# A stick-breaking attention stage: suffix sums from two f32r parts, one diagonal mask, weight low parts on GpSimd

## The reference

```python
z = jnp.einsum('bhqd,bhkd->bhqk', qb, kb)
before = s_idx < t_idx
log_keep = jnp.where(before, jax.nn.log_sigmoid(-z), 0.0)
log_stick = lax.cumsum(log_keep, axis=3, reverse=True) - log_keep
log_w = jax.nn.log_sigmoid(z) + log_stick
w = jnp.where(before, jnp.exp(log_w), 0.0)
outs.append(jnp.einsum('bhqk,bhkd->bhqd', w, vb))
```

## Time and profile before

| | us |
|---|---|
| median of 3 runs (1935.58 to 1937.6) | 1936.41 |
| the profiled execution | 1935.0 |
| its span, first to last instruction | 1933.3 |
| stick-breaking stage in it, first L1332 to the last matmul before gating | 1542.5 to 1662.3 |

### The profile page before, as it was taken

How to read it: one execution, slowest core, us unless ns; L and a number is a source line. 1 busy time by engine, 2 the same in 40 slices (tenths; PEclk the granted TensorE clock), 3 DMA queues, 4 the chain that set the end, 5 groups by cost and what they waited for, 6 DMA issues and landing times.

```text
span 1933.3 us, 25136 instructions
## 1 busy us (share of the span) xinstructions
PE 1873.5 (97%) x8758; PEld 1490.3 (77%) x8758; DVE 1200.1 (62%) x1844; ACT 799.5 (41%) x1258; POOL 34.1 (2%) x60
## 2 busy tenths in 40 slices
PE   9999999879999999999999999999999999899997
PEld 6888888757888888877777778888887777677875
DVE  7777777745677663356565567767533588665444
ACT  6444444424444442244444444444322355543222
POOL 1000000000000000000000000000000000000000
PEclk9999999999999999999999999999999999999998
DMA  5411211102222232132222132222321311122221
GB/s 202 137 55 56 62 56 33 63 26 88 97 97 87 98 116 90 45 120 76 65 65 75 34 120 97 87 98 76 135 90 60 101 33 66 60 98 87 98 85 57
DMA packets 43407, 158.96 MB, mean 82 GB/s; under 512 B 5489, under 2 KB 5764, under 8 KB 43360
## 3 DMA queue, kind: packets, MB, share of 16 engines
q1 hardware_dynamic: 38592, 143.80, 21.8%
q0 software_dynamic: 4336, 14.47, 2.7%
q10 hardware_dynamic: 432, 0.07, 0.0%
HBM read 155.89 MB, written 6.63 MB: 84 GB/s over the span
## 4 chain that ended last, share of the span: by engine, by line
PE 92%; DVE 4%; ACT 2%; issue 1%; DMA 0%; SPq 0%; DVEq 0%; ACTq 0%
PE acc L504 22%; PE acc L505 22%; PE acc L506 22%; PE acc L528 8%; PE pb L643 2%; PE pc L658 2%; PE pa L808 2%; PE pd L829 1%; PE pa L878 1%; PE pd L890 1%; PE pd L647 1%; ACT wsplit L1010 1%; PE pa L605 1%; PE pa L624 1%; DVE wsplit L1460 1%
## 5 line engine op out<-in xcount | busy, mean ns | idle before, releaser
L504 PE MATMUL acc<-xhi,wsplit 128*128 128x512 f32 x1200 | 505.5, 421 | 8.7 <-DVE wsplit L1460 7.7
L505 PE MATMUL acc<-xlo,wsplit 128*128 128x512 f32 x1200 | 476.3, 397 | 0.0
L506 PE MATMUL acc<-xhi,wsplit 128*128 128x512 f32 x1200 | 476.0, 397 | 0.0
L1010 ACT ACTIVATE wsplit<-wraw 128x1024 fp32r<-128x1024 f32 (+1 forms) x252 | 275.1, 1096 | 455.6 <-PE acc L506 428.8
L1460 DVE TENSOR_TENSOR wsplit<-wraw,wsplit 128x1024 fp32r<-128x1024 f32 (+1 forms) x252 | 320.1, 1274 | 160.8 <-ACT wsplit L1010 158.3
L504 PEld LDWEIGHTS acc<-xhi,wsplit 128*128 128x128 f32 x1200 | 226.6, 189 | 71.9 <-issue 14.0
L505 PEld LDWEIGHTS acc<-xlo,wsplit 128*128 128x128 f32 x1200 | 226.9, 189 | 60.3 <-issue 6.2
L506 PEld LDWEIGHTS acc<-xhi,wsplit 128*128 128x128 f32 x1200 | 226.4, 189 | 55.0
L528 PE MATMUL acc<-xhi,wsplit 128*128 128x512 f32 x464 | 158.3, 409 | 0.0
L506 PE MATMUL acc<-hid_hi,wsplit 128*128 128x512 f32 x352 | 139.5, 396 | 0.0
L505 PE MATMUL acc<-hid_lo,wsplit 128*128 128x512 f32 x352 | 139.5, 396 | 0.0
(11 more groups left out here) (330 smaller groups left out, 2741.4 us busy)
## 6 DMA issues: line engine op xcount, KB each, us to landing
wraw<-w SPq DMA_DIRECT2D x220, 512.0 KB, 3.3
wraw<-w SPq DMA_DIRECT2D x32, 704.0 KB, 4.0
bias_dram<-ext_dram POOLq DMA_DIRECT2D x1, 4096.0 KB, 20.2
bias<-bias_dram POOLq DMA_DIRECT2D x8, 512.0 KB, 4.0
crow<-row_dram POOLq DMA_DIRECT2D x8, 256.0 KB, 3.9
brow<-row_dram POOLq DMA_DIRECT2D x8, 256.0 KB, 4.4
outT<-h SPq DMA_DIRECT2D x8, 256.0 KB, 2.2
h<-xT SPq DMA_DIRECT2D x3, 512.0 KB, 8.7
```

The source lines that it names most:

```text
L504: mm(out, whi[:, k, :], a[:, x_at + k, :], start=(k == first), stop=False)
L505: mm(out, whi[:, k, :], b[:, x_at + k, :], start=False, stop=False)
L506: m = mm(out, wlo[:, k, :], a[:, x_at + k, :], start=False, stop=(k == last))
L1010: A(split(s, j, 0), raw(s, j), ACT.Copy).then_inc(w_hi_ready, 1)
```

## The change

- The softplus goes to a dense double buffer `sp` of 2 x 512 columns by unit parity. ScalarE copies it to `sp_hi` (f32r), VectorE writes `sp_lo` = `sp` - `sp_hi`, and the suffix sum is two f32r matmuls, over `sp_hi` and over `sp_lo`, with an f32r copy `suf` of the triangular matrix.
- The diagonal mask with -1e30 is added to `zs` before |z| is taken, in place of after the suffix sum. The softplus of a masked logit is then zero, so the multiplication with `O_BEFORE` goes, and the exponential of unit t - 3 waits for the subtraction itself.
- The low parts of the weight tiles of stick-breaking blocks 1 to 3 and of the gating stage's first group are made by GpSimd in place of VectorE: twelve tiles. VectorE waits for the last of them before the gating stage.
- The gating stage's four table transfers count on one semaphore; who needs one of them waits for all.

```diff
--- before.py
+++ after.py
@@ -41,7 +41,7 @@
 
 C_ID, C_ONE, C_CUM, C_SUF, C_M1, C_INCL2, C_NEGD, C_LEV = 0, 1, 2, 3, 4, 5, 7, 8
 NCONST = C_LEV + len(LEVELS)
-O_ROWS, O_BEFORE, O_NEGD, O_SUF = range(4)
+O_SUF, O_NEGD = 0, 1
 LAST = 96
 
 
@@ -254,7 +254,8 @@
         yb_hi = r.sb("yb_hi", [P, GPP, S], F32R)
         yb_lo = r.sb("yb_lo", [P, GPP, S], F32R)
         second = r.at
-        order = sb("order", [P, 4, P], at=second - S * 4)
+        order = sb("order", [P, 2, P], at=second - S * 4)
+        suf = sb("suf", [P, P], F32R, at=second - P * 4)
         mg_hi = r.sb("mg_hi", [P, KD, S], F32R)
         mg_lo = r.sb("mg_lo", [P, KD, S], F32R)
         ga = r.sb("ga", [P, 2, S])
@@ -266,7 +267,9 @@
         sk_vt = r.sb("sk_vt", [P, 2, 2, NC, P])
         sk_z = r.sb("sk_z", [P, SBP, S])
         zs = r.sb("zs", [P, 2, TRI])
-        sp = r.sb("sp", [P, 2, TRI])
+        sp = r.sb("sp", [P, 2, S])
+        sp_hi = r.sb("sp_hi", [P, 2, S], F32R)
+        sp_lo = r.sb("sp_lo", [P, 2, S], F32R)
         sw = r.sb("sw", [P, 2, TRI])
         sk_o = r.sb("sk_o", [P, S])
         r = Region(second)
@@ -457,7 +460,7 @@
                 pool.wait_ge(acc_free, st["stick_z"].first)
                 moved = ((slice(0, LAST), slice(0, LAST)), (slice(LAST, LAST + 1), slice(P - 1, P)), (slice(LAST + 1, P), slice(LAST, P - 1)))
                 for to, of in moved:
-                    pool.dma_start(order[to, 0:3, :], consts[of, C_SUF:C_NEGD + 1:2, :]).then_inc(ev("tables_landed"), 16)
+                    pool.dma_start(order[to, :, :], consts[of, C_SUF:C_NEGD + 1:C_NEGD - C_SUF, :]).then_inc(ev("tables_landed"), 16)
                 for e in range(2):
                     other = slice(64 - 64 * e, P - 64 * e)
                     pool.wait_ge(ev("heads_zeroed"), 2 * e + 4)
@@ -466,16 +469,23 @@
                     nc.gpsimd.memset(sk_vt[:, e, :, :, other].rearrange("p b t d -> p (b t) d"), 0.0).then_inc(ev("heads_zeroed"), 1)
                 pool.wait_ge(ev("tables_landed"), 64)
                 for to, of in moved:
-                    nc.gpsimd.tensor_copy(order[:, O_SUF, to], order[:, O_ROWS, of]).then_inc(ev("heads_zeroed"), 1)
+                    nc.gpsimd.tensor_copy(suf[:, to], order[:, O_SUF, of]).then_inc(ev("heads_zeroed"), 1)
+                for i in range(1, SBP + 1):
+                    s, n = (st["stick"], i) if i < SBP else (st["sgu"], 0)
+                    for j in range(3):
+                        pool.wait_ge(w_lo_ready, s.number(n, j))
+                        pool.wait_ge(w_hi_ready, s.number(n, j) + 1)
+                        nc.gpsimd.tensor_tensor(split(s, j, 1), raw(s, j), split(s, j, 0).bitcast(F32), ALU.subtract
+                                                ).then_inc(w_lo_ready, 1)
             if "sgu" in stages:
                 pool.wait_ge(ev("ya_lo_ready"), SBP)
                 pool.wait_ge(acc_free, st["sgu"].first)
-                pool.dma_start(wsp[:], w_spat).then_inc(ev("wsp_landed"), 16)
+                pool.dma_start(wsp[:], w_spat).then_inc(ev("sgu_landed"), 16)
                 for e in range(2):
                     src = b_spat.rearrange("(i e) t -> e i t", e=2)[e]
-                    pool.dma_start(bsp[64 * e:64 * e + 64], src.partition_broadcast(64)).then_inc(ev("bsp_landed"), 16)
-                pool.dma_start(lngb[:], ln_gb.partition_broadcast(P)).then_inc(ev("lngb_landed"), 16)
-                pool.wait_ge(ev("wsp_landed"), 16)
+                    pool.dma_start(bsp[64 * e:64 * e + 64], src.partition_broadcast(64)).then_inc(ev("sgu_landed"), 16)
+                pool.dma_start(lngb[:], ln_gb.partition_broadcast(P)).then_inc(ev("sgu_landed"), 16)
+                pool.wait_ge(ev("sgu_landed"), 64)
 
                 nc.gpsimd.memset(wsp[64:P, :, 0:64], 0.0).then_inc(ev("wsp_ready"), 1)
                 pool.wait_ge(ev("wsp_ready"), 1)
@@ -897,11 +907,12 @@
                     if 2 <= step < units + 2:
                         u = step - 2
                         e, k = u % 2, 3 - u % 8 // 2
-                        pe.wait_ge(ev("sp_ready"), u + 1)
+                        pe.wait_ge(ev("sp_lo_ready"), u + 1)
                         if u >= 2:
                             pe.wait_ge(ev("drest"), u - 1)
-                        mm([pb, pc][u % 2][:, 0:(4 - k) * P], order[:, O_SUF, :], sp[:, e, SEG[k]:SEG[k] + (4 - k) * P],
-                           start=True, stop=True).then_inc(ev("suffix_done"), 1)
+                        out, w = [pb, pc][u % 2], (4 - k) * P
+                        mm(out[:, 0:w], suf[:], sp_hi[:, u % 2, 0:w], start=True, stop=False)
+                        mm(out[:, 0:w], suf[:], sp_lo[:, u % 2, 0:w], start=False, stop=True).then_inc(ev("suffix_done"), 1)
                     if step % 8 == 6 and step < units - 8:
                         turn_v(step // 8 + 1)
 
@@ -1340,8 +1351,12 @@
                     if 3 <= step < units + 3:
                         u, e, k = step - 3, (step - 3) % 2, 3 - (step - 3) % 8 // 2
                         g = slice(SEG[k], SEG[k] + (4 - k) * P)
-                        act.wait_ge(ev("dmasked"), u + 1)
+                        act.wait_ge(ev("drest"), u + 1)
                         A(sw[:, e, g], zs[:, e, g], ACT.Exp).then_inc(ev("sw_ready"), 1)
+                    if 1 <= step < units + 1:
+                        u, w = step - 1, (4 - (3 - (step - 1) % 8 // 2)) * P
+                        act.wait_ge(ev("sp_ready"), u + 1)
+                        A(sp_hi[:, u % 2, 0:w], sp[:, u % 2, 0:w], ACT.Copy).then_inc(ev("sp_hi_ready"), 1)
                     if i < SBP - 1 and v in (2, 5, 7):
                         if v == 7:
                             turned_v(i + 1)
@@ -1844,7 +1859,6 @@
                     if j == 2:
                         dve.wait_ge(ev("heads_zeroed"), 11)
                     take(0, j)
-                    low_ahead(s, 0, j, False)
                 units = 8 * SBP
 
                 for step in range(units + 5):
@@ -1856,6 +1870,9 @@
                         u, e, k = step, step % 2, 3 - step % 8 // 2
                         g = slice(SEG[k], SEG[k] + (4 - k) * P)
                         dve.wait_ge(ev("zs_ready"), u + 1)
+                        tt_(zs[:, e, SEG[k]:SEG[k] + P], zs[:, e, SEG[k]:SEG[k] + P], order[:, O_NEGD, :], ALU.add
+                            ).then_inc(ev("dmasked"), 1)
+                        dve.wait_ge(ev("dmasked"), u + 1)
                         stt(sw[:, e, g], zs[:, e, g], -1.0, zs[:, e, g], ALU.mult, ALU.max).then_inc(ev("z_abs"), 1)
                     if 3 <= step < units + 3:
                         u, e, k = step - 3, (step - 3) % 2, 3 - (step - 3) % 8 // 2
@@ -1863,27 +1880,24 @@
                         dve.wait_ge(ev("suffix_done"), u + 1)
                         tt_(zs[:, e, g], zs[:, e, g], [pb, pc][u % 2][:, 0:(4 - k) * P], ALU.subtract
                             ).then_inc(ev("drest"), 1)
-                        dve.wait_ge(ev("drest"), u + 1)
-                        tt_(zs[:, e, SEG[k]:SEG[k] + P], zs[:, e, SEG[k]:SEG[k] + P], order[:, O_NEGD, :], ALU.add
-                            ).then_inc(ev("dmasked"), 1)
                     if 1 <= step < units + 1:
                         u, e, k = step - 1, (step - 1) % 2, 3 - (step - 1) % 8 // 2
-                        g = slice(SEG[k], SEG[k] + (4 - k) * P)
+                        g, w = slice(SEG[k], SEG[k] + (4 - k) * P), (4 - k) * P
                         dve.wait_ge(ev("z_ln"), u + 1)
-                        stt(sp[:, e, g], zs[:, e, g], 0.0, sw[:, e, g], ALU.max, ALU.add).then_inc(ev("sp_whole"), 1)
-                        dve.wait_ge(ev("sp_whole"), u + 1)
-                        x = tt_(sp[:, e, SEG[k]:SEG[k] + P], sp[:, e, SEG[k]:SEG[k] + P], order[:, O_BEFORE, :], ALU.mult)
+                        x = stt(sp[:, u % 2, 0:w], zs[:, e, g], 0.0, sw[:, e, g], ALU.max, ALU.add)
                         if k < 3:
-                            later = slice(SEG[k] + P, SEG[k] + (4 - k) * P)
-                            x = stt(sp[LAST:P, e, later], [pb, pc][u % 2][0:32, 0:(3 - k) * P], cst[LAST:P, C_ID, LAST:LAST + 1],
-                                    sp[LAST:P, e, later], ALU.mult, ALU.add)
+                            x.then_inc(ev("sp_whole"), 1)
+                            dve.wait_ge(ev("sp_whole"), u // 8 * 6 + u % 8 - 1)
+                            x = stt(sp[LAST:P, u % 2, P:w], [pb, pc][u % 2][0:32, 0:w - P], cst[LAST:P, C_ID, LAST:LAST + 1],
+                                    sp[LAST:P, u % 2, P:w], ALU.mult, ALU.add)
                         x.then_inc(ev("sp_ready"), 1)
                     if ahead and v in (2, 5):
                         take(i + 1, v // 3)
-                    if ahead and v in (3, 6):
-                        low_ahead(s, i + 1, v // 3 - 1, i + 1 == SBP - 1)
-                    if 0 < i < SBP and v == 0:
-                        low_ahead(s, i, 2, i == SBP - 1)
+                    if 1 <= step < units + 1:
```

(9 more changed lines are left out.)

## The result

| | before | changed | ratio (95% interval) |
|---|---|---|---|
| median, us | 1936.41 | 1956.32 | 1.0107 (1.0092 to 1.0122) |
| profiled execution, us | 1935.0 | 1958.26 | |
| span, us | 1933.3 | 1956.6 | |
| start of the first logits' copy to start of the last sk_o, us | 119.5 | 140.8 | |

What follows compares the result with a forecast made beforehand. TensorE was taken as the bound (30.1 us a block), with the ScalarE-VectorE ping-pong near. Profiled 1935.0 + 1.5 (loop) + 17 (hold) = 1953.5, with the runs' median 1.4 above the profiled execution: 1955 us; range 1936 to 1963.

Steps and rivals of the forecast that it cites:

- the loop: Stick-breaking stage: ScalarE and VectorE wait on each other each step around sp_hi, 29.8 us a block; about +1.5 us in all.
- the hold: VectorE operations with two SBUF inputs wait for a GpSimd low part, 1.9 us nine times, +17 us; chance 0.52.
- the two passes of the estimate: GpSimd low part: two input streams of 1024 elements read one after the other, some 1.05 us each, 2.1 us together.
- Block 0 and the end: Stick-breaking stage: block 0 unchanged, first three steps staying with TensorE; block 3 +1.5 us and the drain -0.4.
- The drain: End of the stick-breaking stage, unit 31's copy to sk_o: 12.1 us before, 11.4 to 11.9 forecast.
- The block without lows (block 3): Sign of being wrong: if block 3 is longer by more than 3 us, a term of the loop is too small.
- The suffix sums: TensorE, two f32r passes in place of f32: 1.95 us a block saved, 30.1 to 28.2 us.
- No cost elsewhere: Low parts ready in time; the spatial weights' memset delays a GpSimd copy about 1 us of 11 us cover.
- No hold: Rival: VectorE has priority or streams interleave, so only the loop costs; 1938 us, between 1933 and 1942; chance 0.24.
- short hold: Rival: GpSimd reads both streams at once and holds VectorE about 1 us, +8 us in all; 1946 us; chance 0.12.
- TensorE stays the bound: Rival: the loop is under 28.2 us a block and GpSimd holds nothing; faster, 1929.5 us; chance 0.06.
- A longer low: Rival: a GpSimd low part takes 3 us or blocks two VectorE operations, +25 us; 1963 us; chance 0.06.

## Why the prediction was right, point by point

- *The time.* 1955 forecast, 1956.3 measured. Both mechanisms are there. In the stage the trace has +21.4 us where the sum had 18.5: the loop cost 3.3 us more than forecast and the hold 0.4 less. That the medians come within 1.3 us is in part luck.
- *The hold of VectorE by GpSimd.* Forecast 1.9 us nine times, 17 us; measured 15.9 by the medians and 16.6 in the stage. A low took 2.37 us, where the two passes of the estimate gave 2.1 and the estimate from the figure in the Trainium skill's "GPSIMD Engine Reference", section "Elementwise — side-by-side cycle accounting", 2.2. The held masks are 1.9 to 2.2 us longer than 0.29, and eight of the nine steps that hold them 1.5 to 2.0 us longer than without the low parts. The earliest, in block 0, is 1.4 us longer and the step behind it 0.5 shorter; without the low parts ScalarE waits 0.4 us for TensorE in each of these two. The inference from one copy of GpSimd that had waited (0.98 against 0.40 us) to VectorE waiting the other way was the weakest step and held.
- *The loop.* Forecast 29.8 us a block, measured 30.8 without low parts. Step by step, from mask to mask in block 2: 3.84, 2.37, 3.47, 3.46, 3.42, 4.21, 4.81, 5.21 us, where the terms of the sum give about 3.8, 2.4, 3.5, 3.0, 3.4, 4.2, 4.6, 5.0. The largest error is step 3, where ScalarE waited 0.82 us for TensorE's logits (the third of the wait rows of the run without low parts). The prediction had 1 us in all for such steps; these waits are 0.5 to 0.9 us in every block, 3.0 us in all. `sp_hi` took 0.63 us at 512 columns for the 0.60 of the copy it was priced as. `sp_lo` took 0.69, as the softplus.
- *Block 0 and the end.* Forecast nothing and about +1; measured +1.25 and +2.2 (28.24 and 34.4 us against 27.0 and 32.2). In block 0 the first three steps stayed with TensorE, as forecast (2.33, 2.64, 2.76 us in both kernels). The step that failed is that the other five would be the loop's alone: in steps 3 and 4 ScalarE waited another 0.44 and 0.41 us for TensorE's logits. In block 3 the seven steps took 21.7 us for a forecast of 21.6. The drain was mis-sized: 12.7 us, where 11.4 to 11.9 was forecast and the kernel before has 12.1; in it VectorE waited 2.0 us for `sp_hi` and ScalarE 1.6 us for the softplus. With blocks 1 and 2 at +0.65 each the loop costs 4.8 us in the trace, 2.9 (1.2 to 4.6) by the times, for a forecast of 1.5 with bounds -3 and +6.
- *"The block without lows (block 3)".* That reading is wrong: the low part of the cast in a block's step 7 runs in the first step of the next one, so block 3 has one, the ninth (1650.06 to 1652.43 us). The sum counts nine and isn't touched, but the sign of being wrong that hangs on this block has to be read from the run without low parts: +2.2 us, under the 3 that would have spoken against a term.
- *The suffix sums.* As forecast: the second f32r pass follows at a distance of 0.24 us for 512 columns, and the narrow ones are not priced as in f32 either (0.17 us for a pair of 128 columns, 0.22 before). The saving is real, and TensorE waits it away.
- *No cost elsewhere.* The memset of the spatial weights waited 5.5 us for the last of the four transfers, so the copy behind it started 3.8 us later relative to the stage's end than before, not 1; the cover of 11 us held, as TensorE has no wait for that copy.
- *The rivals.* "No hold" and "short hold" fall with the 2.37 us masks, "TensorE stays the bound" with the run without low parts. "A longer low" was right in that lows are longer than 2.1 us, but no mask was followed by a second one held.

## What to carry to other kernels

Work given to an idle engine isn't free if it can hold up the busy one: before moving a two-input operation to GpSimd, look at what VectorE has queued at that moment, and count the first operation there with two SBUF inputs as waiting to the end of GpSimd's instruction, as the nine masks did here. The wait is recorded as a long instruction, not as idle time: look for a mean that is too long for its shape. When a step is added, write down the order of each engine's instructions and look for a loop that closes within a step; its sum, with the hand-overs, is a bound like that of the busiest engine, and it turns every operation that was hidden into a cost. A saving on the bounding engine is worth only the distance to the next bound, here less than nothing.

## What the runs showed that was not expected

TensorE's granted clock fell three times in the changed kernel's stage. Busy time, granted clock and DMA share around the first fall, and inside the other two:

```profile
1613.00:1617.50 4.50, 2.15 (x10) 1.44 (x9) 3.77 (x4) 2.32 (x5) 2.38 (x1) 0.97 0.11 15
1617.50:1620.50 3.00, 2.93 (x6) 2.04 (x7) 2.23 (x6) 1.32 (x5) 0.00 (x0) 0.50 1.01 376
1620.50:1624.00 3.50, 3.50 (x16) 2.76 (x16) 2.71 (x10) 2.34 (x7) 0.00 (x0) 0.98 0.27 109
...
1645.00:1651.00 6.00, 5.89 (x17) 4.41 (x17) 4.24 (x7) 3.69 (x8) 0.94 (x1) 0.50 0.00 0
1655.00:1658.00 3.00, 3.00 (x8) 1.91 (x8) 1.99 (x5) 1.78 (x6) 0.00 (x0) 0.50 0.10 40
```

TensorE had stood idle for 2.43 us up to 1617.57, waiting for the exponential behind a held mask. The granted clock went to 0.50, the lower of its two levels (1.2 GHz), in the last half microsecond of that wait and stayed there for 3.4 us: products came every 0.43 us in place of 0.23. It fell again at about 1644.5 for 6.6 us, after several waits in a row, and at about 1654.8 for 3.4 us, soon after a wait of 1.87 us. The same wait of 2.41 us in block 1, at 1581.24, was followed by no such fall. In the run without low parts the clock is 1.00 in all four blocks; in the kernel with the low parts back on VectorE it is 0.95 in block 2, so a fall doesn't need a held mask. The cost was small, since TensorE had time to spare: block 2 is 0.09 us longer than block 1, and the second and third step of block 3, where the last fall lies, are 0.3 and 0.5 us longer than without the low parts. Why some waits were followed by a fall and others not, these runs don't show.
